# A float32 transformer layer on one core: shifting SBUF places by 32 bytes modulo 512

## The reference

```
mix = jnp.concatenate([y_pool, y_conv, y_dsa, y_nsa], axis=-1)
x = _layernorm(DN_ALPHA * x + mix @ w_out[l], ln1_g[l], ln1_b[l])
gate, up = jnp.split(x @ w_gate_up[l], 2, axis=-1)
x = _layernorm(DN_ALPHA * x + (jax.nn.silu(gate) * up) @ w_down[l], ln2_g[l], ln2_b[l])
```

## The kernel before

| tensor | before | after |
|---|---|---|
| `act` (and the sum s3 within it) | 128 | 224 |
| whole slabs in `w_hi`, `w_lo` | 128 | 224 |
| ring slots | 128 | 192 |
| `raw` (loaded weights) | 128 | 224 |
| `xs_1`, `xs_2`, `xs_4` (block sums, spare slot) | 160 | 224 |
| late pieces | 160 | 192 |
| `h01`, `h23`, `raw_c`, `acc`, `proj` | 160 | 192 |
| `ident` | 128 | 192 |

## Time and profile before

### The profile page before, as it was taken

One profiled execution on the slowest core, in us unless ns is written; L12 is line 12 of the kernel. 1 busy time (PEld: TensorE's weight loads), 2 busy tenths in 40 slices (PEclk: granted clock), 3 DMA queues, 4 the chain that ended last, 5 costly groups with the idle time before them and its releaser, 6 DMA issues.

```text
span 2103.7 us, 32707 instructions
## 1 busy us (share of the span) xinstructions
PE 2066.8 (98%) x12681; PEld 1828.0 (87%) x12681; DVE 1325.4 (63%) x1891; ACT 647.4 (31%) x1027; POOL 389.1 (18%) x187
## 2 busy tenths in 40 slices
PE   8999999999999899999999999999999999999997
PEld 7778888866887799998989999898998989999896
DVE  1069994363113876675857667585766757677588
ACT  2020000354000253342424334243442424334250
POOL 5536666144566300000000000000000000000010
PEclk9999999999999999999999999999999999999999
DMA  6323334300522234242332424233242323334242
GB/s 198 86 77 91 89 99 120 125 21 23 217 91 90 81 90 121 81 122 83 88 121 81 141 62 133 79 110 121 81 131 71 112 90 114 118 85 125 81 130 92
DMA packets 292039, 214.02 MB, mean 102 GB/s; under 512 B 9510, under 2 KB 256102, under 8 KB 289994
## 3 DMA queue, kind: packets, MB, share of 16 engines
q1 hardware_dynamic: 291834, 211.97, 34.0%
q10 hardware_dynamic: 80, 0.13, 0.0%
HBM read 207.76 MB, written 4.19 MB: 101 GB/s over the span
## 4 chain that ended last, share of the span: by engine, by line
PE 94%; DVE 4%; DMA 0%; issue 0%; ACT 0%; POOL 0%; SPq 0%; DVEq 0%; ACTq 0%
PE psum L1108 13%; PE psum L1104 13%; PE psum L1106 13%; PE psum L1145 7%; PE psum L1146 7%; PE psum L1147 7%; PE psum L734 6%; PE psum L736 6%; PE psum L735 6%; PE psum L965 3%; PE psum L967 3%; PE psum L966 3%; PE psum L945 1%; PE psum L883 1%; DVE acc L1796 1%; DVE acc L1802 1%
## 5 line engine op out<-in xcount | busy, mean ns | idle before, releaser
L1106 PE MATMUL psum<-act,w_hi 128*128 128x256 f32 x1344 | 380.2, 283 | 0.0
L1104 PE MATMUL psum<-act,w_hi 128*128 128x256 f32 x1344 | 380.2, 283 | 0.0
L1108 PE MATMUL psum<-act,w_lo 128*128 128x256 f32 x1344 | 380.2, 283 | 0.0
L1864 DVE TENSOR_TENSOR w_lo<-raw,w_hi 128x1024 fp32r<-128x1024 f32 x210 | 257.0, 1224 | 131.8 <-ACT w_hi L1379 131.8
L1864 DVE TENSOR_TENSOR w_lo<-raw_c,w_hi 128x1024 fp32r<-128x1024 f32 x164 | 201.0, 1226 | 177.8 <-ACT w_hi L1379 177.8
L1379 ACT CAST w_hi<-raw 128x1024 fp32r<-128x1024 f32 x212 | 223.1, 1052 | 222.6 <-PE psum L1147 137.2
L1108 PE MATMUL psum<-xs,w_lo 128*128 128x256 f32 x1008 | 283.3, 281 | 0.0
L1104 PE MATMUL psum<-xs,w_hi 128*128 128x256 f32 x1008 | 282.4, 280 | 0.0
L1106 PE MATMUL psum<-xs,w_hi 128*128 128x256 f32 x1008 | 280.3, 278 | 0.0
L1145 PE MATMUL psum<-w_hi,h 128*128 128x512 f32 x672 | 266.6, 397 | 2.4 <-DVE h L1894 2.4
L1146 PE MATMUL psum<-w_hi,h 128*128 128x512 f32 x672 | 266.4, 396 | 0.0
(11 more groups left out here) (229 smaller groups left out, 3276.8 us busy)
## 6 DMA issues: line engine op xcount, KB each, us to landing
raw_c<-in_w_gate_up SPq DMA_DIRECT2D x84, 512.0 KB, 4.2
raw<-in_w_gate_up SPq DMA_DIRECT2D x84, 512.0 KB, 4.7
raw_c<-in_w_down SPq DMA_DIRECT2D x82, 512.0 KB, 4.0
raw<-in_w_in SPq DMA_DIRECT2D x31, 1024.0 KB, 5.7
raw<-in_w_out SPq DMA_DIRECT2D x16, 1024.0 KB, 5.1
proj<-in_x SPq DMA_DIRECT2D x4, 1024.0 KB, 7.9
acc<-in_x SPq DMA_DIRECT2D x1, 4096.0 KB, 12.4
raw<-in_w_gate_up SPq DMA_DIRECT2D x4, 1024.0 KB, 6.2
```

The source lines that it names most:

```text
L1104: nc.tensor.matmul(out_ap, stat_hi[:, cols], mov_hi[:, k, :], start=opens and k == 0, stop=False, skip_group_check=not opens)
L1106: nc.tensor.matmul(out_ap, stat_hi[:, cols], mov_lo[:, k, :], start=False, stop=False, skip_group_check=not opens)
L1108: mm = nc.tensor.matmul(out_ap, stat_lo[:, cols], mov_hi[:, k, :], start=False, stop=k == kh - 1, skip_group_check=not opens)
L1864: nc.vector.tensor_tensor(lo, src, hi.bitcast(F32), ALU.subtract).then_inc(lo_ready, 1)
```

## The change

The tensors of the loop are laid out anew. `w_hi` and `w_lo` become views into one tensor `w_room`: the ring slots start at its beginning, the whole slabs 8 words (32 bytes) further. `xs_1` and `xs_2` become views into `x_room` in the same manner, with the late pieces at its beginning. `act` is declared after `w_room`, and the block sums, h, `s_nat` and the norms' gains are declared in another order. The ring slot of granule `at` is now `at % 4` and not `(at + 2) % 4`.

Since a ring slot now lies in the memory of another slab, the order of slab slots in the transition changes. Slab FF0 + 2 goes to slot 0 and FF0 + 3 to slot 1, and the second token half takes the two slabs in the order of the first one (u = 1, then u = 0). The gate's bank 4 is thus filled second and not first, and `gate(0)` waits for `slab_done` FF0 + 2 in place of FF0 + 1. No engine's list of instructions is put in another order: only operands and this wait differ.

```diff
+        eps = sb("eps", [P, 1])
+        std = sb("std", [P, TT])
+        w_room = sb("w_room", [P, 4 * SLAB + P + SHIFT], F32R)
+        w_hi, w_lo = (w_room[:, SHIFT + at:SHIFT + at + 2 * SLAB].rearrange("p (s n) -> p s n", s=2)
+                      for at in (0, 2 * SLAB + P))
         act = sb("act", [P, 2, KT, SEQ], F32R)
         act_hi, act_lo = act[:, 0, :, :], act[:, 1, :, :]
-        w_hi = sb("w_hi", [P, 2, SLAB], F32R)
-        w_lo = sb("w_lo", [P, 2, SLAB], F32R)
         raw = sb("raw", [P, 2, SLAB])
...
+        x_room = sb("x_room", [P, 4 * SLAB + SHIFT], F32R, feed)
+        xs_1, xs_2 = (x_room[:, SHIFT + at:SHIFT + at + 2 * SLAB].rearrange("p (k a n) -> p k a n", a=2, n=HALF_TOKS)
+                      for at in (0, 2 * SLAB))
...
+        spare_slot = (x_room[:, SHIFT:SHIFT + SLAB], x_room[:, SHIFT + SLAB:SHIFT + 2 * SLAB])
+        late = [(x_room[:, at:at + GRAN], x_room[:, at + GRAN:at + 2 * GRAN]) for at in range(0, 8 * GRAN, 2 * GRAN)]
...
         def ring_hi(at):
-            r = (at + 2) % 4
-            return w_hi[:, r // 2, (r % 2) * GRAN:(r % 2 + 1) * GRAN]
+            r = at % 4
+            return w_room[:, r * GRAN:r * GRAN + GRAN]
...
         def ring_lo(at):
-            r = (at + 2) % 4
-            return w_lo[:, r // 2, (r % 2) * GRAN:(r % 2 + 1) * GRAN]
+            r = at % 4
+            return w_room[:, P + (4 + r) * GRAN:P + (4 + r) * GRAN + GRAN]
...
-            split(1, odd + 16 * (ff_pair + 2), FF0 + 2)
-            split(0, even + 16 * (ff_pair + 2), FF0 + 3)
+            split(1, odd + 16 * (ff_pair + 2), FF0 + 2, dst=(w_hi[:, 0, :], w_lo[:, 0, :]))
+            split(0, even + 16 * (ff_pair + 2), FF0 + 3, dst=(w_hi[:, 1, :], w_lo[:, 1, :]))
...
-                    u = 1 - v if half == 0 else v
+                    u = 1 - v
...
-                    mm = passes(psum[:, 6 + u, :], w_hi[:, 1 - u, cols], w_lo[:, 1 - u, cols],
+                    mm = passes(psum[:, 6 + u, :], w_hi[:, u, cols], w_lo[:, u, cols],
...
             def gate(j):
-                act.wait_ge(slab_done, FF0 + 2 * j + 1)
+                act.wait_ge(slab_done, FF0 + 2 + j)
```

More of the change, by code:

```diff
@@ L95 @@
 GRAN = SLAB // 2
+SHIFT = 8
 HALF_TOKS = SEQ // 2
@@ L142, in build @@
         shift = sb("shift", [P, TT])
-        std = sb("std", [P, TT])
         ident = sb("ident", [P, P])
-        eps = sb("eps", [P, 1])
         mixing = ExitStack()
@@ L179, in build @@
         h01 = sb("h01", [P, 2, 2, SEQ], F32R, feed)
+        s_scope = ExitStack()
+        with s_scope:
+            s_nat = sb("s_nat", [P, 2, GRAN], F32, s_scope)
+        h23 = sb("h23", [P, 2, 2, SEQ], F32R, feed)
+        s2_scope = ExitStack()
+        with s2_scope:
+            below_s2 = sb("below_s2", [P, 2 * SLAB + SHIFT], F32, s2_scope)
+            s2_nat = sb("s2_nat", [P, 2, GRAN], F32, s2_scope)
+        x_room = sb("x_room", [P, 4 * SLAB + SHIFT], F32R, feed)
+        xs_1, xs_2 = (x_room[:, SHIFT + at:SHIFT + at + 2 * SLAB].rearrange("p (k a n) -> p k a n", a=2, n=HALF_TOKS)
+                      for at in (0, 2 * SLAB))
         first_norm = ExitStack()
@@ L188, in build @@
         ln2_bias = sb("ln2_bias", [P, D_MODEL], F32, feed)
[L189 to L197, removed]
         gains, biases = (ln1_gain, ln2_gain), (ln1_bias, ln2_bias)
```

## The result

The changed kernel takes 2080.1 us (median of 4 runs, 2079.07 to 2081.02) against 2105.89 us before (4 runs). The ratio is 0.9871, 95% interval 0.9858 to 0.9885: 25.8 us faster. The forecast was 2087.1 us, with a range of 2081 to 2096. The direction was right and the range just missed.

A forecast was written before the change was run, and what follows sets the result against it. TensorE, busy 98% of the span, was taken as the bound. Terms -8.0 (products on act), -12.2 (down), -0.1 (spare slot) and +1.6 (gate) sum to -18.7 us, giving 2087.1 us, range 2081 to 2096.

The forecast's parts named there:

- What bounds it, and that distance decides: Whole kernel: as long as its matmuls; operand distance modulo 512, not absolute place, sets the time between matmul starts.
- nothing gains: Rival: pace differences come from the instructions, not operand places; only the gate's wait, +1.6 us, is left; 2107 us, chance 0.05.
- Products on act go from distance 0 to +32, where the block sums are: 4032 product matmuls over 42 chunks: 0.19 us saved per chunk, -8.0 us, bounds 0 and -20.
- Block sums ... the distance stays +32, 0 and 0, so nothing: Block sums, late pieces and slabs keep their distances and move only in absolute place: no change in time.
- More than forecast: Rival: all products at one distance reach the best third's pace, and down gains a whole -13; about -7, 2080 us, chance 0.07.
- Down: Down matmuls on the ring go from distance -32 to 0: 1.2 us for each of ten groups, -12.2 us.
- The gate's wait: Transition: `gate(0)` waits for the second slab, delaying `turn_s(1)`, `combine(2)` and `turn_s(2)`: +1.6 us, bounds 0 and 5.
- The other moves at nothing: Waits in the loop stay covered by 2.2 us of slack; transposes' changed pairs at most 0.6 us either sign: costed at nothing.

The follow-up runs named there:

- 64 bytes lower: The changed kernel with small tensors packed so that each large tensor lies 64 bytes lower, all distances kept: 2080.05 us.
- h alone: The changed kernel with h and the late pieces 32 bytes further, so down matmuls on the ring return to distance -32: 2091.21 us.
- The first experiment: The changed kernel with `act` and the whole slabs back at the ring's place, products on `act` at distance 0, block sums still at +32: 2096.56 us.
- the mirror: The changed kernel with the block sums at the ring's place (distance 0) and `act` kept at +32: 2096.17 us.
- the break: The kernel with `act` at distance 0 plus one TensorE drain before the first block-sum product of each of 42 chunks: 2112.43 us.
- the gate behind: The changed kernel with ACT's `gate(0)` moved behind `s_high_parts(0)`: 2078.7 us, and 2078.44 us when run once more.

## Why the prediction was wrong where it was

- *What bounds it, and that distance decides*: right. With 512 columns distance 0 was fast and 32 bytes slow in every kernel, with 256 columns distance 0 was slower than +32, and 64 bytes lower changed no pace. The rival "nothing gains" is out: h alone is worth 11.1 us. The Trainium skill's rule in "TensorE: Matmul & The Clock Gate", section "Step-by-step: what each phase is for", that loading the next weights takes nothing from the running matmul, would have given that rival; the measurements decide against it here.
- *Products on act go from distance 0 to +32, where the block sums are*: the mechanism held, the size failed. I took the block sums' 117.9 ns as the pace of distance +32. It was the pace of +32 beside products at 0. The failed step is this price: the term measured -13.0 us, not -8.0.
- *Block sums ... the distance stays +32, 0 and 0, so nothing*: failed for the block sums, -3.6 us. This step assumed that a pace belongs to a pair of operands. The first experiment, the mirror and the break show that it also belongs to what ran ahead.
- *More than forecast* named this outcome (2080 us), with 0.07, and its idea, one distance for all products, was the right one. Its number is partly luck. Its "about -7" doesn't follow from its terms, since 2 ns on three quarters of 7056 products is already 10.6 us. In the table the products gave 8.6 us more than forecast, and the 1.7 us of the attention part, which the change didn't cause, took some of that back. The trace of before held a hint: the three lines on block sums had unequal printed durations, 280, 278 and 281 ns, and I read that as a spread of forms, not as a pattern that repeats over three matmuls. The low end of the range, 2081, cut that rival off; a bound of -20 us stood in the text for the products and was not kept for the range.
- *Down*: -12.2 forecast, -12.3 in the trace, 11.1 us by the experiment's times. The sum rounded 1.23 us a group to 1.2; unrounded it is -12.5.
- *The gate's wait*: +1.6 forecast, +1.65 in the trace and nothing left of it with the gate behind. `combine(2)` was forecast at 5.4 us (733.1 to 738.5) and took 5.44. The trace agrees with the reason given: POOL's subtraction runs from 733.09 to 737.68, `combine(2)` starts at 734.45 and ends at 739.89, 2.2 us after POOL, and its twin of 2.36 us had no POOL beside it. The exclusion that the Trainium skill states in "SBUF — State Buffer", section "Who interferes with whom", fits this. On PE `turn_s(1)` cost 1.2 us (forecast 1.3) and `turn_s(2)` 0.4 (forecast 0.3 to 0.6).
- *The other moves at nothing*: right. No product waits in the loop.

## What to carry to other kernels

Where TensorE is the bound and a stationary and a moving operand both come from SBUF, try the difference of their places modulo 512 bytes as a tuning constant, per matmul form; read it from start-to-start distances, since the busy share shows nothing. Don't take the pace of one group in a mixed stream as what that kind of placement gives: it can be inherited from the group ahead, and a uniform stream, or one behind another kind of matmul or a break, can show a different one. A tensor that moves for such a reason can change which slot is filled first; look at what stands behind the wait that moves with it.

## What the runs showed of the hardware

- A matmul of 256 columns with one weight load per matmul runs at 119.9 ns with both operands at the same place modulo 512, and at 116.7 ns with the moving one 32 bytes above. With 512 columns it is the other way round: 226.8 ns at the same place, 233.3 ns 32 bytes apart.
- Two steady paces at one distance: 116.7 and 117.8 ns, each held over at least 69 matmuls. The slow one stands behind a stream at distance 0; behind a drain of the pipeline either came (33 of 42 fast, 9 slow), and in the kernel of the mirror experiment the fast one behind 512-column matmuls (24 matmuls, 11 times). What in the engine holds the phase was not resolved.
- A drain of TensorE between two products cost 0.45 us.
- The attention part ended at 522.66 and at 524.59 us in two kernels with the same program up to there, at a granted clock of 1.00 and 0.93 from 420 to 445 us; what makes the clock differ is open.
